# The block attention's query tiles and memory-key tiles in the wide form, in a float32 two-block transformer kernel

## The reference

```python
k, v = jnp.split(rms_norm_2(x, kv_norm) @ w_kv, 2, axis=-1)
k = apply_partial_rope(k.reshape(bsz, seq, N_HEADS, HEAD_DIM_2), cos, sin)
q = apply_partial_rope((h @ w_q).reshape(bsz, seq, N_HEADS, HEAD_DIM_2), cos, sin)
...
s_own = jnp.einsum("bhqd,bhkd->bhqk", q_c, k_own).astype(jnp.float32) * scale
s_own = jnp.where((kpos[None, :] <= qpos[:, None])[None, None], s_own, -jnp.inf)
p = jax.nn.softmax(jnp.concatenate([s_sel, s_own], axis=-1), axis=-1)
...
k, v = jnp.split(mem_n @ w_kv, 2, axis=-1)      # the memory's keys and values
```

## Time and profile before

| | |
|---|---|
| time, median of 3 runs | 1233.29 us (1232.48 to 1233.83) |
| time of the profiled execution | 1232.41 us |
| its span | 1230.6 us |
| TensorE busy | 1223.9 us, 99% of the span |
| VectorE busy | 937.8 us, 76% |
| ScalarE busy | 663.9 us, 54% |

### The profile page before, as it was taken

The page is one execution under the profiler, slowest core; times in us unless marked ns, Lnnn a source line. Parts: engine busy times, 40 slices in busy tenths (PEclk is TensorE's granted clock), DMA queues, the critical chain, the costliest instruction groups (busy, mean ns, idle before and its releaser), DMA issues.

```text
span 1230.6 us, 18136 instructions
## 1 busy us (share of the span) xinstructions
PE 1223.9 (99%) x7434; PEld 1093.0 (89%) x7434; DVE 937.8 (76%) x1310; ACT 663.9 (54%) x883; POOL 32.9 (3%) x23
## 2 busy tenths in 40 slices
PE   9999999999999999999999999999999999999998
PEld 8888889978888888888898888889998898888887
DVE  7887766869777858988778777669968667877744
ACT  6666544556655544446556555454655555555532
POOL 0000000000000000540000000000000000000000
PEclk9999999999999999999999999999999999999999
DMA  8565665235455673556346555644445534555560
GB/s 319 200 216 180 226 206 171 72 136 199 177 184 192 209 229 111 194 186 220 123 161 215 202 177 195 215 168 162 148 145 184 185 137 145 200 202 177 199 208 35
DMA packets 52114, 221.74 MB, mean 180 GB/s; under 512 B 4640, under 2 KB 6976, under 8 KB 31552
## 3 DMA queue, kind: packets, MB, share of 16 engines
q1 hardware_dynamic: 51744, 220.32, 51.8%
q10 hardware_dynamic: 288, 0.27, 0.1%
HBM read 219.52 MB, written 1.05 MB: 179 GB/s over the span
## 4 chain that ended last, share of the span: by engine, by line
PE 93%; DVE 4%; issue 1%; ACT 1%; DMA 0%; SPq 0%; DVEq 0%; ACTq 0%
PE bank L428 40%; PE bank L486 17%; PE bank L448 8%; PE bank L432 7%; PE bank L473 5%; PE bank L442 4%; PE bank L531 2%; PE bank L823 2%; DVE wt L1365 1%; PE bank L508 1%; PE bank L534 1%; PE bank L858 1%; PE bank L513 1%; PE bank L841 0%; DMA raw<-weights 0%
## 5 line engine op out<-in xcount | busy, mean ns | idle before, releaser
L1365 DVE TENSOR_TENSOR wt<-raw,wt 128x2048 fp32r<-128x2048 f32 x202 | 464.2, 2300 | 68.0 <-ACT wt L988 67.6
L988 ACT ACTIVATE wt<-raw 128x2048 fp32r<-128x2048 f32 x202 | 385.8, 1910 | 114.7 <-PE bank L432 62.4
L428 PE MATMUL bank<-xn,wt 128*128 128x512 f32 x1280 | 311.7, 393 | 0.0
L428 PEld LDWEIGHTS bank<-xn,wt 128*128 128x128 f32 x1280 | 235.3, 188 | 47.1 <-issue 1.1
L428 PE MATMUL bank<-h,wt 128*128 128x512 f32 x1004 | 244.3, 392 | 0.0
L428 PEld LDWEIGHTS bank<-h,wt 128*128 128x128 f32 x1004 | 183.0, 188 | 34.6 <-issue 0.4
L486 PEld LDWEIGHTS bank<-xn,wt 128*128 128x128 f32 x1360 | 174.0, 191 | 7.6 <-DVE wt L1365 1.6
L486 PE MATMUL bank<-xn,wt 128*128 128x256 f32 x1360 | 177.4, 283 | 0.3 <-DVE wt L1365 0.2
L1485 DVE TENSOR_TENSOR scratch<-bank,rest 128x512 f32<-128x512 f32 x98 | 67.7, 691 | 86.2 <-ACT rest L1000 86.1
L1075 ACT ACTIVATE h<-scratch 128x256 fp32r<-128x256 f32 x88 | 36.8, 418 | 156.9 <-DVE scratch L1525 156.9
L448 PE MATMUL bank<-xn,wt 128*128 128x512 f32 x432 | 103.2, 391 | 0.0
(11 more groups left out here) (237 smaller groups left out, 1142.1 us busy)
## 6 DMA issues: line engine op xcount, KB each, us to landing
raw<-weights SPq DMA_DIRECT2D x158, 1024.0 KB, 4.9
raw<-weights SPq DMA_DIRECT2D x86, 512.0 KB, 4.9
raw<-weights SPq DMA_DIRECT2D x12, 256.0 KB, 4.7
k_t<-mem_t SPq DMA_DIRECT2D x2, 1024.0 KB, 7.0
raw<-weights SPq DMA_DIRECT2D x8, 128.0 KB, 4.1
out_t<-work SPq DMA_DIRECT2D x4, 256.0 KB, 2.3
x<-x_t SPq DMA_DIRECT2D x3, 256.0 KB, 5.2
v_s<-fourier SPq DMA_DIRECT2D x2, 256.0 KB, 5.4
```

The lines of the kernel that those rows point to most:

```text
L428: return pe.matmul(out, hi, a.rearrange("p a s -> p (a s)"), start=first, stop=False, skip_group_check=True)
L988: act.activation(wt[t % RING][:, 0], raw[t % RING][:], ACT.Copy).then_inc(weight_hi, 1)
L1365: dve.tensor_tensor(wt[t % RING][:, 1], raw[t % RING][:], wt[t % RING][:, 0].bitcast(F32), ALU.subtract).then_inc(weight_lo, 1)
```

## The change

Six of the fourteen moba tiles, the four of queries (q0 to q3) and the two of memory keys (m0, m1), become wide. The keys k0 to k3, the values and w_in stay narrow. Queries are no longer copied out by ScalarE: ScalarE copies the second half to SBUF and VectorE adds it to the first, into `q_t`. For the memory's keys ScalarE's copy and VectorE's addition are new, and the multiplication by `r_m` is done on SBUF afterwards. A query's bank pair is now free after VectorE's addition, not after ScalarE's copy.

```diff
-NARROW = ("w_in", "moba")
+def narrow_tile(name, j):
+    return name == "w_in" or name == "moba" and MOBA[j][0] in "kv"
...
-        _by = "copied_out" if _name == "moba" and MOBA[_j][0] in "qv" else "drained"
+        _by = "copied_out" if _name == "moba" and MOBA[_j][0] == "v" else "drained"
...
-        if _name not in NARROW:
+        if not narrow_tile(_name, _j):
             REST[_name, _j] = len(RESTS)
             RESTS.append((_name, _j))
...
-                    square_tile(t, out, src, ks=ks, narrow=kind in NARROW, **more)
+                    square_tile(t, out, src, ks=ks, narrow=narrow_tile(kind, j), **more)
...
-                if kind == "moba":
+                if kind == "moba" and what == "v":
                     src = pair_banks(kind, j)
-                    if what == "q":
-                        act.wait_ge(tile_done, FIRST[kind] + j + 1)
-                        act.activation(q_t[:, pair(i), :], src[:, :, 0:S], ACT.Copy).then_inc(copied_out, 1)
...
+                elif narrow_tile(kind, j):
+                    return
                 elif what != "v":
                     rest(kind, j)
...
-                if name in NARROW:
+                if narrow_tile(name, j):
                     dve.wait_ge(tile_done, FIRST[name] + j + 1)
                     dve.tensor_tensor(dst, pair_banks(name, j)[:, :, 0:S], both(r), ALU.mult).then_inc(drained, 1)
                     return
```

More of the change, by code:

```diff
@@ L753, in part @@
                 if what == "v":
-                    value_tile(t, out, src, ks=ks, beside=more.get("beside", {}), narrow=kind in NARROW)
+                    value_tile(t, out, src, ks=ks, beside=more.get("beside", {}), narrow=narrow_tile(kind, j))
                 else:
-                    square_tile(t, out, src, ks=ks, narrow=kind in NARROW, **more)
+                    square_tile(t, out, src, ks=ks, narrow=narrow_tile(kind, j), **more)
             def pieces(kind, n, i, ready):
@@ L1008, in rest_part @@
                 what, i = PARTS[kind][j]
-                if kind == "moba":
+                if kind == "moba" and what == "v":
                     src = pair_banks(kind, j)
-                    if what == "q":
-                        act.wait_ge(tile_done, FIRST[kind] + j + 1)
-                        act.activation(q_t[:, pair(i), :], src[:, :, 0:S], ACT.Copy).then_inc(copied_out, 1)
[L1014 to L1019, removed]
+                    act.wait_ge(tile_done, FIRST[kind] + j + 1)
+                    act.wait_ge(factor, SPREAD_AT["mix1"])
+                    for n in range(NT):
+                        e = act.activation(v_s[:, n, 2 * P * i:2 * P * (i + 1)], src[:, n, 0:S], ACT.Copy, scale=col_x[:, n:n + 1])
+                    e.then_inc(copied_out, 1)
+                elif narrow_tile(kind, j):
+                    return
                 elif what != "v":
```

## The result

The changed kernel takes 1234.91 us (median of 21 runs, 1234.32 to 1235.36), the kernel before 1232.69 us in the same comparison (median of 21, 1232.06 to 1234.78). The ratio is 1.0015, 95% interval 1.0009 to 1.0022, so the change costs 1.1 to 2.7 us. The ratio is within the 0.2% that I named beforehand (the interval's upper end is just above it), the median is inside the range, and on the slower side as forecast. The profiled execution took 1234.47 us with a span of 1232.7 us, 2.1 more than before; TensorE's busy time hardly changed (1224.2 us in place of 1223.9), and the granted clock stayed at 1.00.

A forecast was written before the change was run, and what follows sets the result against it. TensorE was taken as the bound, with VectorE nearly full in the block attention. The 1.14 us gain became a 1.2 us loss through waits for VectorE: 1232.41 + 1.2 = 1233.6 profiled, median 1234.5 (0.9 above), range 1232.0 to 1236.3.

The forecast's parts named there:

- within 0.2%: Whole kernel: time within 0.2% (2.5 us) of the kernel before, chance 0.84.
- TensorE gains 1.14 us: Six wide tiles on TensorE: 12 ns saved per matmul pair, 0.19 us a tile, 1.14 us in all.
- An addition makes VectorE 0.73 us late: VectorE's queue at the queries: 0.55 us late after q0, 0.73 more for each of q1 to q3, 2.74 in all.
- The waits of TensorE: Block attention: TensorE's shift followed place by place, with waits at head 0's scores, q2's weight lo, heads 2 and 3.
- Head 3: L863 of head 3: TensorE waits 1.20 us for VectorE's `rest` of head 2, shift +1.42; the place that decides.
- The step that failed: Behind head 3: VectorE has idle time, lateness ends, no further waits; shift +1.16 at the end after the memory keys' saving.
- my list: TensorE's forecast shifts in the block attention: -0.05, +0.05, +0.22, then +1.42 at head 3 and +1.16 at the end.
- much smaller: Sign in the profile after: VectorE's idle time before `rest` of head 4 shrinks much; no size given.
- The memory keys: m0 and m1: added emptying steps cost nothing, m0's first piece gains nothing, the other 22 pairs save 0.26 us.
- first rival: Block attention: VectorE's lateness never reaches TensorE, giving -1.14 us, a median of 1232.15; chance 0.12.
- second: Query additions: VectorE also waits for ScalarE's copy, +3.3 us at the end, a median of 1236.6; chance 0.12.
- third: TensorE's wide tiles: weight loads are the real limit, fewer loads give -11.5 us, 1221.8; chance 0.02.

The follow-up runs named there:

- two kernels: Against the kernel before: only m0, m1 wide, m0's weights split earlier, ratio 0.9997; q0, q1, m0, m1 wide with VectorE and ScalarE work reordered, ratio 0.9992.
- the last experiment: Kernel before with only m0 and m1 wide and m0's weight split ahead of the normalising of head 6: 99.73 us locally, ratio 0.9997.
- the two reorderings: Changed kernel with VectorE's `rest` of heads 1, 2 ahead of k3, q3 and ScalarE's v2 copies ahead of head 6's exponentials: 100.36 us locally, +0.26 against before.

## Why the prediction was right, and what it missed

I had forecast a loss of 1.2 us and a median of 1234.5. Measured were +1.99 us locally, 2.2 between the medians, and a median of 1234.91. The direction, the cause (VectorE's lateness reaches TensorE) and "within 0.2%" held; the loss was nearly twice the forecast. That the two medians lie only 0.4 us apart is partly luck. My base was a median of three runs, 0.9 above the profiled execution; the median of 21 is only 0.3 above it, and these 0.6 us hid most of the missing term. Step by step:

- *TensorE gains 1.14 us.* The wide tiles take 5.56 us as forecast. The gain shows where no wait takes it back: two kernels have it locally (-0.37 and -0.58 us), though in time neither is told from no change. The Trainium skill ("TensorE: Matmul & The Clock Gate", section "Wait — 56ns, not 53.3ns?") has 2.5 ns beside the columns of each warm matmul; the trace's 120 and 228 ns are 13 and 15 above their columns at 2.4 GHz, and 10 ns for each matmul less is what the last experiment measured. The measurement decides.
- *An addition makes VectorE 0.73 us late, and the lateness adds up to 2.74.* Measured 2.6 to 2.7.
- *The waits of TensorE.* Scores of head 0: forecast 0.33, and there the row at 856.47 is 0.25 behind the end of q1's stretch (854.30 and 16 x 0.12). Weight lo of q2: forecast 0.29; the row at 867.37 is 0.11 behind its stretch (863.61 and 16 x 0.228) and 0.10 longer than before (2.18 for 2.08), 0.21 in all. Head 1: no wait, as forecast. Head 2: forecast start 891.07, measured 891.02. Head 3: 898.94, measured 898.89. (The changed kernel's stretch began 0.08 us later than before, so these starts are 0.13 us earlier than forecast.)
- *The step that failed:* "Behind it VectorE has idle time again and follows TensorE, so that the lateness ends there", with L863 of heads 4 to 7 "released by nothing". The term for head 4 was missing. Its rows were there to read; ScalarE's timeline of the kernel before has

```profile
901.81 0.46 ACT L1165 ACTIVATE scratch<-bank,small,q_scale 128x128 f32<-128x128 f32 x1 [2.56 <-DVE small L1690]
...
902.80 0.83 ACT L1018 ACTIVATE v_s<-bank,col_x 128x256 f32<-128x256 f32 x2
```

  and TensorE's

```profile
898.18 0.49 PE L841 MATMUL bank<-con,scratch 128*128 128x128 f32 x3
...
904.20 0.82 PE L863 MATMUL bank<-scratch,v_s 128*128 128x256 f32 x4
904.85 0.49 PE L841 MATMUL bank<-con,scratch 128*128 128x128 f32 x3
```

  The copy of v2 ended at 903.63, 0.57 us ahead of its reader (L863 of head 4, at 904.20), behind exponentials that wait for VectorE's maximum. With the change both are 2.7 us later:

```profile
904.49 0.46 ACT L1166 ACTIVATE scratch<-bank,small,q_scale 128x128 f32<-128x128 f32 x1 [2.64 <-DVE small L1691]
...
905.48 0.83 ACT L1017 ACTIVATE v_s<-bank,col_x 128x256 f32<-128x256 f32 x2
```

  The copy ends at 906.31 and TensorE starts at 906.37. In the local measure (the changed kernel's starts less 0.08) the transposes behind L863 of head 3 come 1.36 us later than before (898.18 to 899.62), those of head 4 2.19 us later (904.85 to 907.12), and the end 1.99; my list had +1.42, +1.42 and +1.16. So the missing term is 0.83 us at head 4, of which some 0.1 is that L866 itself takes longer after a wait. The rest of the sum was 0.06 too high at head 3 and 0.06 too good for the memory keys.

  The idle time of VectorE "behind it" was not where I put it. Behind head 3 it idles 1.16 us at 902.94, again for exponentials that wait for its own maximum, and that gap stayed. The first idle time that can take the lateness up is the one before the `rest` of head 4, which waits for TensorE's L863 of head 4 and so lies behind it. Before, it was

```profile
905.47 0.42 DVE L1706 TENSOR_TENSOR h<-bank,h 128x256 fp32r<-128x256 f32 x1 [1.77 <-ACT h L1211]
```

  and with the change

```profile
907.74 0.42 DVE L1707 TENSOR_TENSOR h<-bank,h 128x256 fp32r<-128x256 f32 x1 [1.37 <-ACT h L1212]
```

  I had written "much smaller" for this idle time; it shrank by 0.40 us, since TensorE itself came 2.2 us late. I had followed VectorE's direct hand-overs to TensorE, and not the instructions of ScalarE that are queued behind something of VectorE's.
- *The memory keys.* Nothing waited for their two emptying steps, and the first ten pairs gained nothing, as forecast: from the first weight hi of m0 to L866 of head 5 it is 3.67 us (909.54 to 913.21), before 3.66.
- *The rivals.* The lateness did reach TensorE (first rival). VectorE never waited for ScalarE's copy of a query (second). Weight loads are not the limit (third). Over tile q0, where nothing waits, the stretches (columns as above) are before and with the change

```profile
844.98:850.74 5.76, 5.76 (x50) 5.76 (x49) 5.69 (x9) 2.64 (x3) 0.00 (x0) 1.00 0.01 4
```

```profile
844.98:850.74 5.76, 5.76 (x36) 5.11 (x35) 5.69 (x9) 2.64 (x3) 0.00 (x0) 1.00 0.00 0
```

  The loads are a third fewer and busy 5.11 us in place of 5.76, and the tile takes 5.56 us in place of 5.76. The Trainium skill ("Perfetto Trace Analysis", section "Identifying the Most-Contended Engine") names the busy share of weight loads, beside the share of the peak rate, as the measure of nearness to TensorE's limit. By it the wide tile is further from the limit, while its time is the shorter one; the trace does not agree here.

The runs also show how the loss follows the lateness: with 2.0 us of it in place of 2.7 the loss is 1.3 us, with 1.3 us it is 0.8, and with 2.7 us and the two reorderings 0.3.

## What to carry to other kernels

When an engine's queue is full, price an instruction added to it as lateness of everything behind it, and look for the smallest slack, not for the engine's mean busy share. Follow the lateness through the other engines' queues as well: what is queued there behind an instruction that waits for the late engine is late too, and a copy that waits for nothing itself can so become the last to arrive. Two waits for one lateness lie behind each other: removing either alone gave 0.05 and 0.9 us, both together 1.7.

## What the runs showed of the hardware

A pair of 256-column matmuls into one bank costs 240 ns and one of 512 columns 228 ns at the granted clock of 1.00, although the narrow form has half as many weight loads again (48 against 32 a tile) and these fill 12.92 of 13 us of a stretch: a record of weight loads busy all the time did not mean that fewer loads would make it faster in proportion. TensorE started 0.06 us after ScalarE's copy ended (906.31 to 906.37) and 0.14 us after VectorE's rest did (898.75 to 898.89). The four matmuls of L866 take longer when they start behind a wait: 0.73 us to the next row at head 3 (898.89 to 899.62) and 0.75 at head 4 (906.37 to 907.12), against 0.65 before (904.20 to 904.85). So each wait cost about 0.1 us beyond itself; no run shows why.
